# A DVE add placed ahead of a weight tile's low part, and a ScalarE square ahead of its high part, in the second out-projections of two feed-forward layers

## What is computed

```python
def conv_glu_ffn(h, w_in, conv_w, conv_b, w_out):
    u = h @ w_in                                  # 1024 -> 2 x 2816
    up = jnp.pad(u, ((0, 0), (CONV_WIDTH - 1, 0), (0, 0)))
    u = sum(conv_w[k] * up[:, k:k + S] for k in range(CONV_WIDTH)) + conv_b
    gate, val = jnp.split(u, 2, axis=-1)
    return (jax.nn.gelu(gate, approximate=True) * val) @ w_out   # 2816 -> 1024
...
    x = x + rms_norm(f, ffn_post_g[layer])
```

## Time and profile before

| | us |
|---|---|
| median of 3 runs | 2486.6 |
| lowest and highest of them | 2482.49, 2488.43 |
| the profiled execution | 2491.49 |
| its span, first to last instruction | 2489.8 |
| PE busy | 2344.2 (94% of the span) |
| DVE busy | 1489.8 (60%) |
| ACT busy | 1097.9 (44%) |
| POOL busy | 455.4 (18%) |
| mean granted TensorE clock | 0.970 of full |

### The profile page before, as it was taken

The page is one execution under the profiler, slowest core; times in us unless marked ns, Lnnn a source line. Parts: engine busy times, 40 slices in busy tenths (PEclk is TensorE's granted clock), DMA queues, the critical chain, the costliest instruction groups (busy, mean ns, idle before and its releaser), DMA issues.

```text
span 2489.8 us, 34962 instructions
## 1 busy us (share of the span) xinstructions
PE 2344.2 (94%) x12834; PEld 1972.0 (79%) x12834; DVE 1489.8 (60%) x2173; ACT 1097.9 (44%) x1768; POOL 455.4 (18%) x448
## 2 busy tenths in 40 slices
PE   8999998888899999879798999999999989999998
PEld 8888887767788788767588888888877768988887
DVE  5785787857578768768835423427666742532433
ACT  5653553535545433543254412326457752431331
POOL 0120222323322212135410000010024421000001
PEclk9999999899999999989899999999999999999999
DMA  5355452212235454443122222222221212222222
GB/s 202 135 184 183 181 181 97 93 60 86 101 120 189 157 185 176 154 160 144 71 84 85 93 92 101 92 85 87 104 69 36 71 35 102 86 100 101 94 91 68
DMA packets 56349, 282.52 MB, mean 113 GB/s; under 512 B 7996, under 2 KB 19008, under 8 KB 28336
## 3 DMA queue, kind: packets, MB, share of 16 engines
q1 hardware_dynamic: 34144, 213.85, 23.9%
q0 software_dynamic: 12560, 58.80, 6.8%
q10 hardware_dynamic: 9536, 8.39, 1.0%
HBM read 265.15 MB, written 15.86 MB: 113 GB/s over the span
## 4 chain that ended last, share of the span: by engine, by line
PE 76%; DVE 14%; ACT 4%; issue 3%; POOL 1%; DMA 0%; SPq 0%; DVEq 0%; ACTq 0%; POOLq 0%
PE ps L481 23%; PE ps L482 22%; PE ps L483 22%; DVE w_lo L1858 3%; ACT w_hi L1127 1%; DVE v L2500 1%; DVE tg L1923 1%; POOL sqsum L2797 1%; PE ps L1062 1%; PE ps L1031 1%; PE ps L810 1%; PE ps L1033 1%; PE ps L1032 1%; DVE small L2099 1%; DVE x L1949 1%
## 5 line engine op out<-in xcount | busy, mean ns | idle before, releaser
L481 PE MATMUL ps<-h_hi,w_hi 128*128 128x512 f32 (+1 forms) x2016 | 744.1, 369 | 25.7 <-DVE w_lo L1858 11.1
L1858 DVE TENSOR_TENSOR w_lo<-raw,w_hi 128x1024 fp32r<-128x1024 f32 x386 | 501.7, 1341 | 417.9 <-ACT w_hi L1127 417.7
L482 PE MATMUL ps<-h_lo,w_hi 128*128 128x512 f32 (+1 forms) x2016 | 734.2, 364 | 0.0
L483 PE MATMUL ps<-h_hi,w_lo 128*128 128x512 f32 (+1 forms) x2016 | 733.6, 364 | 0.0
L1127 ACT ACTIVATE w_hi<-raw 128x1024 fp32r<-128x1024 f32 x386 | 386.7, 1052 | 408.1 <-PE ps L483 406.2
L481 PEld LDWEIGHTS ps<-h_hi,w_hi 128*128 128x128 f32 x2016 | 389.7, 193 | 92.0 <-issue 17.0
L481 PE MATMUL ps<-a_hi,w_hi 128*128 128x512 f32 (+1 forms) x1164 | 427.3, 367 | 26.6 <-DVE f L2316 11.7
L482 PEld LDWEIGHTS ps<-h_lo,w_hi 128*128 128x128 f32 x2016 | 390.0, 193 | 57.5 <-issue 1.0
L483 PEld LDWEIGHTS ps<-h_hi,w_lo 128*128 128x128 f32 x2016 | 389.9, 193 | 57.1
L482 PE MATMUL ps<-a_lo,w_hi 128*128 128x512 f32 (+1 forms) x1164 | 424.4, 365 | 0.0
L483 PE MATMUL ps<-a_hi,w_lo 128*128 128x512 f32 (+1 forms) x1164 | 424.1, 364 | 0.0
(11 more groups left out here) (395 smaller groups left out, 2697.8 us busy)
## 6 DMA issues: line engine op xcount, KB each, us to landing
raw<-weights_dram SPq DMA_DIRECT2D x161, 1024.0 KB, 4.7
ada_w<-ada_dram POOLq DMA_DIRECT2D x48, 1024.0 KB, 5.1
raw<-weights_dram SPq DMA_DIRECT2D x32, 704.0 KB, 3.9
par<-par_dram SPq DMA_DIRECT2D x8, 1152.0 KB, 7.7
par_dram<-plane POOLq DMA_DIRECT2D x10, 512.0 KB, 3.8
tab<-tab_dram SPq DMA_DIRECT2D x8, 512.0 KB, 5.7
x_tok<-x_rows_dram SPq DMA_DIRECT2D x4, 512.0 KB, 6.2
x<-x_in_dram SPq DMA_DIRECT2D x1, 2048.0 KB, 14.2
```

Of the source, the lines that this page charges most:

```text
L481: nc.tensor.matmul(dst, w_hi[:, o:o + P], rhs_hi, start=start, stop=False)
L482: nc.tensor.matmul(dst, w_hi[:, o:o + P], rhs_lo, start=False, stop=False)
L483: return nc.tensor.matmul(dst, w_lo[:, o:o + P], rhs_hi, start=False, stop=last)
L1858: nc.vector.tensor_tensor(w_lo[:, o], raw[:, o], w_hi[:, o].bitcast(f32), SUB).then_inc(w_split, 1)
```

## The change

Both `ffn{layer}_out_b` loops, DVE's and ScalarE's, get `splits="last"`. Nothing is added or taken away. In steps 0 to 5 of either layer DVE's add of tile s stands ahead of the low part of tile s+2, and ScalarE's square of tile s ahead of the high part of tile s+2. The callbacks stay behind both. The rows on PE, POOL and SP stay the same.

```diff
@@ ScalarE, ffn(layer)
-                    tiles(f"ffn{layer}_out_b", squares, (out_chunk, 1), (C["free_dve"], 1), (C["sq"], 1), then=tables5 if layer else rope_sines, last=2)
+                    tiles(f"ffn{layer}_out_b", squares, (out_chunk, 1), (C["free_dve"], 1), (C["sq"], 1), splits="last", then=tables5 if layer else rope_sines, last=2)
@@ DVE, ffn(layer)
-                    tiles(f"ffn{layer}_out_b", add_out, (out_chunk, 1), then=more_turns5 if layer else constants5, last=2)
+                    tiles(f"ffn{layer}_out_b", add_out, (out_chunk, 1), splits="last", then=more_turns5 if layer else constants5, last=2)
```

## The result

The changed kernel took 2490.94 us, the median of 20 runs (2486.78 to 2495.09), beside 2484.85 us for the kernel before on the same chips (20 runs, 2482.49 to 2492.97). The ratio is 1.0020 with a 95% interval of 1.0012 to 1.0028: **0.2% slower**, 3 to 7 us; the two medians differ by 6.1. The forecast was 2486.2, that is 0.4 us less than before, which counts as no change. The measured time lies inside the range of 2481 to 2494, but the kernel became slower, by about the 5 us that the text had set as the bound. That forecast and result lie only 4.7 us apart is in part the base: the forecast was counted from 2486.6, the median of 3 runs, and 20 runs give 2484.85.

What follows compares the result with a forecast made beforehand. DVE was taken to bound layer 0, ScalarE and DVE in turns layer 1. Layer 0's loss of 6.3 us less layer 1's gain of 6.7 gave -0.4 on 2486.6, so 2486.2 us, range 2481 to 2494.

Steps and rivals of the forecast that it cites:

- What bounds layer 0: Layer 0's loop: DVE is the bound, without idle time before; the new order idles it 1.8 us every step.
- The term of 6.3 us: Layer 0: tile 7 starts at 422.1 instead of 415.81, 6.3 us later.
- The same clock fall: Layer 0, tile 7: PE's wait grows from 2.65 to about 4 us, with an unchanged clock fall behind it.
- Layer 1 up to tile 7: Layer 1's loop: tile 2 starts 1.1 us later, tiles 3 and 4 earlier, tile 7 at 1061.5 instead of 1066.95.
- Layer 1's last step: End of layer 1: last table's store issued at 1063.05, DVE let go 3.10 us behind, second halves 6.7 us earlier.
- The slower one: Both layers: POOL's delay stays on DVE's constants and tables, 8.0 us more, 2494; chance 0.15.
- The faster one: Both layers: PE's waits on the add just go, 16.5 us gained, 2470; chance 0.05.
- The third: PE hides DVE's round trip in layer 0, so only layer 1 counts: 6.7 us gained, 2480; chance 0.08.

Runs made afterwards that it cites:

- DVE's half alone: Against the kernel before, only DVE's add goes ahead of the low part, in both layers; ScalarE keeps the old order: 2478.25 us, ratio 0.9973.
- the layer-0 kernel: Against the kernel before, both engines take the new order in layer 0 only: 2491.05 us, ratio 1.0022.
- the load held: Against the changed kernel, SP holds one s5_in weight load until table 7 is stored: 2484.15 us, ratio 0.9997 to the kernel before.
- the hold: Against the kernel before, in the old order, SP holds the load of tile 1 of s5_in until table 7 is stored: 2487.28 us, ratio 1.0007.

## Why the prediction was right and wrong, step by step

**What bounds layer 0: right.** DVE did, and the change lengthened its round. Idle time ahead of `w_lo` was put at 1.8 us and is 1.70; `w_lo` meets POOL's add for 0.25 us, put at 0.3; the constants got their delay back as put (2.67 and 2.68 for 2.69). The add of step 5 was put at 418.1 and came at 417.92, tile 7 at 422.1 and came at 421.79. The rule of the Trainium skill on the shared port ("SBUF — State Buffer", Who interferes with whom), by which the order of issue decides who waits, held in both directions. In the changed kernel POOL's add is first and `w_lo` waits; with DVE's half alone a half of `w_lo` can be first, and POOL's add is then stretched, from 1.3 us to as much as 2.01:

```profile
1036.56 2.01 POOL L2797 TENSOR_TENSOR sqsum<-sqsum,sq 128x512 f32<-128x512 f32 x1 [5.95 <-ACT sq L1159]
```

**The term of 6.3 us: right in kind, slightly short.** Tile 7 is 6.0 us late, and at the sum behind the second halves it is 6.4, in the layer-0 kernel 7.2. PE's wait there is 5.01 us and not the 4 that were put, and the clock stays low longer behind it: 4.4 us in the changed kernel and 6.2 in the layer-0 kernel, where it was 3.4 before. "The same clock fall" was not something to count on: the old wait of 2.65 us had one in two executions of the old order and none in a third.

**Layer 1 up to tile 7: right.** Less the 6.67 us by which this loop began late, tile 2 starts at 1023.5 (put at 1023.5), tile 3 at 1033.2 (1032.9), tile 7 starts at 1061.4 (1061.5), the last store is issued at 1063.07 (1063.05). Only the waits on the way were put wrong: behind the one of 1.90 us at tile 3 the clock fell, PE itself became late, and tile 7, put at a wait of 1.3 us, came with next to none.

**Layer 1's last step: wrong, and this is the error.** That the second halves wait for the last table's store was right. But "DVE is let go 3.10 us behind it" took the landing time of the store over from the old order, in which no load was issued just ahead of it. It was 6.93 us, 3.8 more. The wait of 4.83 us that came of it also brought the clock down. Granted clock in two stretches of the changed kernel behind it (columns as in the earlier trace rows):

```profile
1077.00:1079.00 2.00, 1.85 (x8) 1.86 (x9) 0.42 (x2) 1.86 (x3) 1.24 (x2) 0.50 0.04 8
1079.00:1081.00 2.00, 2.00 (x12) 2.00 (x11) 0.00 (x0) 0.17 (x1) 0.23 (x1) 0.50 0.00 0
```

From the start of the second halves to the sum it takes 15.95 us and took 14.03: 1.9 us more, for which the sum had nothing. 6.7 - 3.8 - 1.9 = 1.0, the gain measured. So the sum is 6.4 - 1.0 = 5.4 us slower, where the prediction had 6.3 - 6.7; the ratio gives 5.0 and the medians 6.1. With the load held, 7.0 us came, where 6.7 had been forecast. The trace of before could have told me: no row of the prediction shows an issue of SP's, though the text itself says that `w_lo` releases SP's load, and the change moves `w_lo`'s end. By the new order `w_lo` (it starts 1.09 us behind the start of `w_hi` and takes 2.6) ends some 0.6 us ahead of the issue of the table's store (`w_hi` takes 2.0, the table 2.3); the collision follows from rows that were there.

**The rivals.** None named this mechanism. The slower one (POOL's delay stays on DVE) fell: the products take 2.7 us. Its time, 2494, is nearer to the measured 2491 than the forecast is, by a mechanism that is not there. The faster one, all waits on the add gone for nothing, fell too: `w_lo` took the add's place. The third, that only layer 1 pays out, is not what happened: layer 0 lost its 6.4 us. DVE's half alone comes close to it in time (7.7 us faster), as layer 0 then costs nothing.

## What to carry to other kernels

When an operation moves, follow everything that its end releases, to the queue that issues the next load, and compare those issue times with the stores that something waits for: a landing time read from the old order holds only if the same transfers are in flight. Two engines that make two parts of one thing need not change order together. Only the engine whose consumer was waiting (here DVE's add) had to put it first; the other's square had slack, and putting it ahead of the high part made a chain of four steps across two engines inside the round of the bound engine, at 7.2 us in layer 0.

## What the runs showed of the hardware

A store of 512 KB that landed 2.6 us after its issue by itself took 6.7 when a load of 1 MB had been issued 0.37 us before it on another engine's queue, and the load itself took 5.9 us instead of 4.8: the smaller transfer paid most. With the load issued 1.15 us before it (DVE's half alone) the store took 6.1, with 3.4 us between them 2.9. In the changed kernel four more table stores were issued 0.4 us behind such a load and took 5.9 to 6.7 us; no engine's idle time ends with those.

PE's idle times of 3.77 us and more in these two loops were each followed by a granted clock of 0.50; behind the one of 4.83 us it lasted some 4 us. Shorter ones were not told apart by their length. An idle time of 1.66 us was followed by no fall (the granted clock is 1.00 from 388 to 392 in the changed kernel), one of 1.90 by one, with the stretch from 1041 to 1043 of the changed kernel behind it:

```profile
1041.00:1043.00 2.00, 2.00 (x6) 1.56 (x5) 1.93 (x4) 1.60 (x4) 0.00 (x0) 0.50 0.48 87
```

One of 2.65 us had a fall behind it in the kernel before, and one of 2.64 at the same place none with the hold; one of 3.20 at tile 7 of layer 1 had one in the kernel before, and one of 3.16 at the same place none in the layer-0 kernel. So what a single such wait costs through the clock, some 1.5 us here, differs between executions of the same code.
